# Order of the convolution, the latent heads and the attentions in two hybrid mixers

## The reference

```
z = rmsnorm(x, mix_norm) @ w_in               # 512 tokens x 2680 columns, split into 15 parts
y_a = dsa_mixer(aq, ak, av, iq, ik, iw, ...)  # an index scores keys, the top 128 per query are kept,
                                              # then softmax attention over those (4 heads of 64)
y_b = gla_mixer(bq, bk, bv, bg, br, ...)      # gated linear attention in chunks
y_c = conv_mixer(cu, ...)                     # h = a * sigmoid(gate); 31-tap causal depthwise
                                              # convolution over 256 channels; rmsnorm; silu
y_d = mla_mixer(dcq, dckv, dkpe, ...)         # latent attention: up-projections, head norms, rope
x = x + concat(y_a, y_b, y_c, y_d) @ w_out
```

## Time and profile before

| | us |
|---|---|
| median of 3 runs | 4438.44 (4437.38 to 4439.28) |
| the profiled execution, whole | 4426.43 |
| the profiled execution, span of the core | 4425.2 |
| first mixer, first projection to the end of its attentions | 2452.2 to 2803 |
| second mixer, the same | 3633.2 to 3984 |

### The profile page before, as it was taken

The page is one execution under the profiler, slowest core; times in us unless marked ns, Lnnn a source line. Parts: engine busy times, 40 slices in busy tenths (PEclk is TensorE's granted clock), DMA queues, the critical chain, the costliest instruction groups (busy, mean ns, idle before and its releaser), DMA issues.

```text
span 4425.2 us, 47206 instructions
## 1 busy us (share of the span) xinstructions
PE 4112.5 (93%) x19301; PEld 3236.6 (73%) x19301; DVE 2267.8 (51%) x3544; ACT 1362.8 (31%) x2134; POOL 149.5 (3%) x294
## 2 busy tenths in 40 slices
PE   7659999999999999999999977999999999589999
PEld 6648887666678888887878764788778777467877
DVE  5745898777724444443332488433233325764331
ACT  3243322333333333332221332422232223333221
POOL 8000000000000000000000001000000000100000
PEclk9679999999999999999999986999999999789999
DMA  3002354555566666662333220133323322102332
GB/s 110 1 12 87 110 145 129 164 183 184 183 190 189 190 190 190 190 190 87 95 96 86 62 69 1 53 95 95 100 77 95 96 81 61 46 1 86 95 95 72
DMA packets 253336, 473.56 MB, mean 107 GB/s; under 512 B 15856, under 2 KB 138896, under 8 KB 250944
## 3 DMA queue, kind: packets, MB, share of 16 engines
q1 hardware_dynamic: 253120, 470.53, 35.1%
HBM read 399.96 MB, written 70.52 MB: 106 GB/s over the span
## 4 chain that ended last, share of the span: by engine, by line
PE 79%; DVE 14%; ACT 3%; POOL 2%; issue 1%; DMA 0%; DVEq 0%; ACTq 0%; POOLq 0%; SPq 0%
PE ps L353 23%; PE ps L355 23%; PE ps L354 23%; DVE arena L2656 2%; POOL arena L1139 2%; DVE arena L1825 2%; PE ps L456 1%; PE ps L2223 1%; DVE arena L1139 1%; DVE wlast L344 1%; DVE arena L2751 1%; DVE arena L1821 1%; DVE arena L1822 1%; PE ps L2251 1%; PE ps L2226 1%
## 5 line engine op out<-in xcount | busy, mean ns | idle before, releaser
L344 DVE TENSOR_TENSOR wlast<-wraw,wlast 128x1024 fp32r<-128x1024 f32 x408 | 499.0, 1227 | 799.9 <-ACT wlast L334 799.4
L353 PE MATMUL ps<-XH,wlast 128*128 128x512 f32 (+1 forms) x1904 | 785.4, 412 | 0.7 <-DVE XL L482 0.7
L354 PE MATMUL ps<-XL,wlast 128*128 128x512 f32 (+1 forms) x1904 | 755.4, 397 | 0.0
L355 PE MATMUL ps<-XH,wlast 128*128 128x512 f32 (+1 forms) x1904 | 754.0, 396 | 0.0
L334 ACT ACTIVATE wlast<-wraw 128x1024 fp32r<-128x1024 f32 x408 | 429.4, 1056 | 459.7 <-PE ps L355 444.0
L344 DVE TENSOR_TENSOR wtwo<-wraw,wtwo 128x1024 fp32r<-128x1024 f32 x210 | 258.1, 1230 | 416.9 <-ACT wtwo L334 416.6
L355 PEld LDWEIGHTS ps<-XH,wlast 128*128 128x128 f32 x1904 | 360.3, 189 | 86.5
L353 PEld LDWEIGHTS ps<-XH,wlast 128*128 128x128 f32 x1904 | 360.9, 190 | 74.4 <-issue 3.6
L354 PEld LDWEIGHTS ps<-XL,wlast 128*128 128x128 f32 x1904 | 361.7, 190 | 70.4
L353 PE MATMUL ps<-XH,wtwo 128*128 128x512 f32 (+1 forms) x944 | 383.8, 407 | 0.7 <-DVE XL L482 0.7
L354 PE MATMUL ps<-XL,wtwo 128*128 128x512 f32 (+1 forms) x944 | 368.4, 390 | 0.0
(11 more groups left out here) (460 smaller groups left out, 6542.2 us busy)
## 6 DMA issues: line engine op xcount, KB each, us to landing
wraw<-in_ut SPq DMA_DIRECT2D x128, 512.0 KB, 4.2
wraw<-in_v SPq DMA_DIRECT2D x128, 512.0 KB, 4.0
wraw<-in_ffn_gate SPq DMA_DIRECT2D x88, 512.0 KB, 3.5
wraw<-in_ffn_up SPq DMA_DIRECT2D x88, 512.0 KB, 3.5
wraw<-in_ffn_down SPq DMA_DIRECT2D x88, 512.0 KB, 3.5
acts<-arena SPq DMA_DIRECT2D x128, 256.0 KB, 4.5
gates<-arena SPq DMA_DIRECT2D x16, 2048.0 KB, 9.0
arena<-gates SPq DMA_DIRECT2D x32, 1024.0 KB, 8.3
```

What stands on the lines that cost most here:

```text
L344: ve.e.tensor_tensor(W.items[n][8], W.rawof(n), W.items[n][7], ALU.subtract).then_inc(*ve.up("wlo", n))
L353: mm(out, lh, rh, start=start, stop=False)
L354: mm(out, lh, rl, start=False, stop=False)
L355: return mm(out, ll, rh, start=False, stop=stop)
```

## The change

Four things change, in `plan_mixer`, in the memory of `Mixer.__init__`, in the generators and in the two lists.

1. The projections come in the order cu0, cu2, iq0, iq1, ik, cu1, cu3, aqk and so on: the values and gates of the convolution's first half first.
2. The convolution goes half by half: 31 taps of half 0 (steps c0 to c7), then 31 of half 1 (c8 to c15), each tap waiting for the one before it. c0 may be called from p1 on and takes two steps a round until p4; half 1 starts after p6, with one step a round.
3. The first list runs until p and h are done. The convolution's steps c20 and c21 are called in the first two rounds of the second list; x stands at step 26 by then. In the second list b begins when c is done, and x goes on only when d has passed step 8.
4. QD, KD and the rotary scratch go to the memory lent by the weight ring; the squares QSQ and KSQ to kTd and qTd; UKV and GT to the place of btmp; UQ behind the convolution's scratch. LLa, LLd, PTa, PTd lie over the convolution's memory, so that both attentions' exponentials on ACT wait for the last convolution step (`cn`), and attention a's for the latent queries too (`uqd`).

```
 def plan_mixer(k, l):
+    for m in (0, 2):
+        plan_T(k, ("cu", l, m), w2, 1848 + 128 * m)
     for m in range(2):
         plan_T(k, ("iq", l, m), w2, 768 + 128 * m)
     plan_T(k, ("ik", l), w2, 1024)
-    for m in range(4):
+    for m in (1, 3):
...
+        self.QSQ, self.KSQ = (x.rearrange("p a b -> p (a b)")[:, 0:1536] for x in (self.kTd, self.qTd))
+        L1.at -= 1024
+        self.UKV = L1(512)
+        self.GT = [[L1(4, 16) for _ in range(4)] for _ in range(2)]
...
+        ar.at = at_c
+        LLa, LLd = ([ar(2, 512) for _ in range(2)] for _ in range(2))
+        PTa, PTd = ([ar(512) for _ in range(2)] for _ in range(2))
...
+        e0.at = 4096
+        self.QD, self.KD = e0(4, 4, 96), e0(4, 4, 96)
+        self.RT = [e0(4, 4, 16) for _ in range(4)]
...
-        needs = {"c": 7, "x": 3, "h": 8}
+        needs = {"c": 2, "x": 5, "h": 8}
-        while any(done[b] < steps[b] for b in "pch"):
-            for b in "pxxh" if done["p"] < 7 else "pcxch":
+        while any(done[b] < steps[b] for b in "ph"):
+            for b in "pcc" if done["p"] < 5 else "pcxxh":
+                if b == "c" and done["c"] >= 8 and done["p"] < 7:
+                    continue
...
     def ve_conv(self):
             ve.after().tensor_tensor(self.H[:, m, 32:544], self.CU[:, m, :], self.CU[:, 2 + m, :],
-                                     ALU.mult).then_inc(*ve.up("ch", l, m))
-        for j in range(31):
-            for m in range(2):
+                                     ALU.mult).then_inc(*ve.up())
+            for j in range(31):
...
-                    ve.wait_ge(*at("ct", l, j - 1, m))
-                    v.scalar_tensor_tensor(self.AC[:, m, :], src, wc, self.AC[:, m, :], ALU.mult,
-                                           ALU.add).then_inc(*ve.up("ct", l, j, m))
+                    ve.after().scalar_tensor_tensor(self.AC[:, m, :], src, wc, self.AC[:, m, :], ALU.mult,
+                                                    ALU.add).then_inc(*ve.up())
...
     def order2(self):
-            if done["x"] >= 12 + 9 * min(max((done["a"] - 5) // 4 + 1, 0) // 2, 3):
+            if (done["a"] < 4 or done["c"] == steps["c"]) and done["x"] >= 12 + 9 * min(max((done["a"] - 5) // 4 + 1, 0) // 2, 3):
                 step("a")
-            if done["d"] != self.d_free or done["a"] > 4:
+            if done["d"] != self.d_free or (done["a"] > 4 and done["c"] == steps["c"]):
                 step("d")
-            step("b")
-            if done["b"] * steps["d"] < done["d"] * steps["b"]:
+            step("c")
+            if done["c"] == steps["c"]:
                 step("b")
-            step("x")
+                if done["b"] * steps["d"] < done["d"] * steps["b"]:
+                    step("b")
+            if done["d"] > 8:
+                step("x")
...
     def ac_a(self):
+        ac.wait_ge(*at("cn", l, 1))
+        ac.wait_ge(*at("uqd", l, 3))
         yield from self.att_a.ac()
...
     def ac_d(self):
-        ac.wait_ge(*at("dTd", l, 3, 1))
+        ac.wait_ge(*at("cn", l, 1))
         yield from self.att_d.ac()
```

More of the change, by code:

```diff
@@ L2336, in __init__ @@
         self.csq, self.crs = ar(2, 512), ar(512)
+        at_t = ar.at
         self.tmp = ar(4, 4, 64)
@@ L2370, in __init__ @@
                               (self.IDR[:, 0, :], self.MR[:, i, 0:nk], 0)], ("m", l))
[L2372 to L2376, removed]
-        self.TRI, self.ZH = ar(128), ar(128, dt=HF)
[L2378 to L2382, removed]
+        e0.at = 4096
+        self.QD, self.KD = e0(4, 4, 96), e0(4, 4, 96)
+        self.RT = [e0(4, 4, 16) for _ in range(4)]
+        e0.at = 0
+        ar.at = at_t
+        self.UQ = ar(2, 384)
+        self.TRI, self.ZH = ar(128), ar(128, dt=HF)
         self.dsq, self.drs = self.csq, self.crs
@@ L2419, in order1 @@
         assert done["x"] >= 12
-        self.done_x = done["x"]
+        self.done_x, self.done_c = done["x"], done["c"]
         return out
@@ L2425, in merged1 @@
             next(gens[b], None)
-        for b in "pch":
+        for b in "ph":
             assert next(gens[b], "end") == "end", b
@@ L2430, in pe_proj1 @@
         k, l, XH, XL = self.k, self.l, self.XH, self.XL
+        for m in (0, 2):
+            pe_proj(k, ("cu", l, m), XH, XL, 0, 5, parts=("xL", self.norm_n))
+            yield
         for m in range(2):
-            pe_proj(k, ("iq", l, m), XH, XL, 0, 5, parts=("xL", self.norm_n))
+            pe_proj(k, ("iq", l, m), XH, XL, 0, 5)
             yield
@@ L2508, in toks @@
             ac.note("tks", key)
+        for m in (0, 2):
+            even(m // 2, ("cu", l, m), self.CU[:, m])
+            yield
         for m in range(2):
@@ L2521, in ac_proj1 @@
         yield
-        for m in range(4):
-            even(m, ("cu", l, m), self.CU[:, m])
+        for m in (1, 3):
+            even(m // 2, ("cu", l, m), self.CU[:, m])
             yield
@@ L2564, in odd @@
                 ve.note("pj", key)
+        for m in (0, 2):
+            odd(m // 2, ("cu", l, m), self.CU[:, m])
+            yield
         for m in range(2):
@@ L2570, in ve_proj1 @@
         yield
-        for m in range(4):
-            odd(m, ("cu", l, m), self.CU[:, m])
+        for m in (1, 3):
+            odd(m // 2, ("cu", l, m), self.CU[:, m])
             yield
@@ L2622, in ac_conv @@
             a(self.CU[:, 2 + m, :], self.CU[:, 2 + m, :], ACT.Sigmoid).then_inc(*ac.up("cgate", l, m))
-        for _ in range(16):
-            yield
-        ac.wait_ge(*at("conv", l))
+            for _ in range(8):
+                yield
+        ac.wait_ge(*at("conv", l, 1))
         ac.wait_ge(*at("dss", l))
@@ L2795, in order2 @@
     def order2(self):
-        steps = {"a": self.n_a, "d": self.n_d, "b": self.n_b, "x": 12 + 27}
+        steps = {"a": self.n_a, "d": self.n_d, "b": self.n_b, "x": 12 + 27, "c": 22}
         done = dict.fromkeys(steps, 0)
-        done["x"] = self.done_x
+        done["x"], done["c"] = self.done_x, self.done_c
         out = []
@@ L2824, with merged2 @@
     n_b = 5 + 4 * 11 + 4 + 1
-    def merged2(self, gens, index):
-        gens["x"] = index
+    def merged2(self, gens):
         for b in self.order2():
@@ L2934, in ac_d @@
             a(self.QD[:, i].rearrange("p h e -> p (h e)"), o, ACT.Copy, scale=r).then_inc(*ac.up("qd", l, i))
-            a(self.dtmp[:, i].rearrange("p h e -> p (h e)"), o, ACT.Square, scale=r).then_inc(*ac.free(("uq", l, i)))
+            a(self.QSQ[:, 384 * i:384 * i + 384], o, ACT.Square, scale=r).then_inc(*ac.free(("uq", l, i)))
             ac.note("dhsq", l, i)
@@ L3324, in sp @@
         k, l = self.k, self.l
+        for m in (0, 2):
+            load(k, ("cu", l, m))
         for m in range(2):
```

42 lines of the change are left out of this document (19 added, 23 removed).

## The result

| | before | after |
|---|---|---|
| median of the runs beside each other | 4437.91 us (4433.86 to 4439.28, 6 runs) | 4420.95 us (4418.07 to 4425.13, 6 runs) |
| profiled execution | 4426.43, span 4425.2 | 4420.54, span 4419.3 |
| ratio after to before | | 0.9963, 95% interval 0.995 to 0.9976 |

The change makes the kernel faster by 0.37%, 17 us where 30 were forecast: inside the range, at 57% of the gain. A later comparison gave the same ratio (0.9963, 0.995 to 0.9977).

What follows compares the result with a forecast made beforehand. In each mixer DVE is idle early and owes work late, which holds PE up twice. A net gain of 15 us a mixer, 30 in all, takes the median from 4438.4 to 4408 us; range 4388 to 4428.

Steps and rivals of the forecast that it cites:

- Part 1: Last projection: the 10.84 us PE idle and low-clock matmuls behind it go, 14.2 us less 2.5, so it comes 11.7 earlier.
- term of 2.5 us: Last projection: loss set against the 14.2 us, as x2 to x5 stand behind ACT's sigmoid or aqk evacuations.
- Rival B: Index scores stuck behind DVE's chained taps in p6 to p10: 15.5 us lost, gain about 0, 4438 us; chance 0.08.
- The price of the chained taps: Convolution on DVE: 60 taps cost 0.12 us more each, 7.1 us, covered by DVE's idle time before 2600.
- Part 2: After the last projection: DVE comes free for the next stage at 2622.9 instead of 2635.36, gain 12.4 us.
- Part 3: Stretch to first latent scores: 62.8 us instead of 74.3, including 7 for bare waits; scores come 24 us earlier.
- Rivals A and D: A: front's waits all bare, 5 us a mixer, 4428, chance 0.12. D: full clock or covered waits, 25, 4388, chance 0.12.
- Part 4: First latent scores to last mask: 42.6 us instead of 33.6, mask 15 us earlier; net gain 15 us a mixer.
- PE's lead (+3): At the last mask: PE stands up to three rounds further on in the list, worth 0 to 6 us, taken as 3.
- the clock (-3): Behind the last mask: some 6 us of full-speed work at half clock, costing 3 us net, between 0 and 9.
- wrong in part 4 if PEclk is under 0.9 for more than 10 us: Sign of failure behind the last L2767, one of three; the forecast fails as a whole if two hold.

Runs made afterwards that it cites:

- the kernel with the filler behind the mask: Kernel after plus twelve 256-column products that compute nothing, ahead of the gated attention's first product behind the last mask: 4427.64 us, 0.9982 of before.
- the kernel without deferral: Kernel after, but the selection (x) goes on from the second list's first round instead of waiting for step 8 of d: 4427.86 us, 0.9989 of before.
- The kernel with the third bank: Kernel after with three PSUM banks for the index's scores and four (instead of five) for the projections: 4408.14 us, 0.9937 of before.
- the fourth with the bank: Kernel after with three index banks, selection not put off, and matmuls that compute nothing in the attentions' front and behind the last mask: 4428.14 us, 0.9987 of before.

## Why the prediction was right in kind and half in size

**Part 1, right in mechanism, its term of 2.5 us mis-sized.** The idle of 10.84 us is gone and L2622 takes half the time, as said; so are the late gates. But the last projection came only 4.1 / 4.7 us earlier instead of 11.7. "Against it I set 2.5 us" for x2 to x5 behind ACT's other work: 14.2 less 4.1 / 4.7 is about 10. I had looked at the waits alone, and they are small (4.1 us, 2.8 before). It is the clock. These are marks 10 to 160 of mixer one, before and after:

```profile
2451.67:2601.67 150.00, 143.06 (x757) 115.11 (x755) 94.66 (x151) 55.92 (x95) 2.28 (x3) 0.98 0.26 74
```

```profile
2455.97:2605.97 150.00, 142.76 (x707) 114.69 (x706) 112.02 (x177) 56.03 (x92) 0.88 (x3) 0.92 0.28 80
```

PE is busy as long in both (143.1 and 142.8 us) and issues 50 matmuls fewer. A mean clock of 0.92 for 0.98 over 150 us is about 9 us of full-speed work less, of the 10 that are missing; 28.7 of these microseconds, from 2555.0, ran at 0.82. The low stretches lie among the index's matmuls and their 0.69 us waits; that the waits bring the clock down fits the rows but isn't shown. Rival B's waits behind the taps did not occur. And 4.5 of the 10 us are not fixed by the code ahead: the kernel with the filler behind the mask has the same code up to there and a last projection at 177.2.

**The price of the chained taps, right.** 0.78 us a tap as read from one pair of rows, and about 6 us of the 7.1 where the cover is missing. The Trainium skill (VectorE: DVE Perf Modes, The DRAIN you can't avoid) says of eight copies that a semaphore after each costs nothing extra. Here every tap signals in both orders, so this isn't the same comparison: what costs 0.12 us a tap is waiting for the operation just before it instead of the one before that.

**Part 2, wrong by what part 1 lost.** (A double round by its own terms is 2.51 us and not 2.45, which is 0.3 us over five of them.) DVE's split at 2635.36 came 4.9 us earlier by the marks instead of 12.4. The late projection left DVE idle for 10.69 us before bq's copy, ahead of work that was ready, and that idle is where its 7.5 us are.

**Part 3, right and a little better.** From there to the latent scores 60.6 us for the 62.8 forecast: so the bare waits cost about 5 of the 7 I took. The gates alone are a poorer mark: 1.2 us earlier in mixer one, since the convolution's last step (1.4 us) and a wait of 1.68 us for the gates' product now stand between the split and them. With part 2's loss the scores came 18.7 / 22.6 us earlier instead of 24. Rivals A and D are out.

**Part 4, the mask right within the loss, the clock's price mis-sized.** The last mask came 8.5 / 12.8 us earlier for 15. Behind it the prediction had PE's lead (+3) and the clock (-3) cancel. From last mask to last product the kernel before takes 61.0 us, the one after 64.0 / 69.2: 3 and 8 us lost. The gated attention's first product parts the two terms. It comes 2.3 us behind the mask, for 4.5 before: PE's lead is worth 2.2 us. From there the same 315 matmuls take 61.7 / 67.0 us for 56.5: the clock costs 5.2 / 10.5 us, where I took 3 and at most 9. The clock is 0.50 for 13.7 us behind the last mask in mixer one and for 25.5 us in mixer two, so the line "wrong in part 4 if PEclk is under 0.9 for more than 10 us" came true in both; it is the only sign of being wrong that did. A hole of 6.6 / 7.6 us stands there because L3235 is queued on DVE behind the last mask. That the loss is the clock's doing, and not DVE's, two things show: DVE is busy 19.9 us in that stretch in every kernel, and with the filler it takes 56.4 us again in both mixers. That the hole is what brings the clock down isn't shown, for the kernel without deferral has no such hole in mixer one and 0.67 there. The Trainium skill (TensorE: Matmul & The Clock Gate, Part 1) says that the throttled state is the default and that activity releases it; the trace agrees as far as that, with 0.50 where PE had just stood idle and 1.00 after it had worked on.

**The sum.** Mixer one: 8.5 - 3.0 = 5.5 us; mixer two: 12.8 - 8.2 = 4.6; forecast 15 each. Nearly all of the shortfall is the granted clock in two places and what follows from the first: the 2.5 us of part 1 were about 10, and the 3 us of part 4 were 5.2 and 10.5. The profiles' mixers give 10 us and the medians 17 in both comparisons; the 7 us between I can't place. The stretches outside the mixers vary by 9 us from one execution of a program to the next, so two single profiles can't place them. By the mixers alone the change gave a third of the forecast; that the program's time lies inside the range owes 7 us to something that I did not predict.

**The best version.** The kernel with the third bank has the lowest median, 4408.1 (0.9937), then 4410.1 and 4411.1, both with the bank too. Its interval just overlaps that of the kernel after (0.9954 against 0.995), and the fourth with the bank, with all fillers and no deferral, had 4428. I would take it, for its time and not for a mechanism I can show.

## What to carry to other kernels

When a reorder trades one long idle of TensorE for several short waits, price the matmuls behind each short wait at the low clock too: here stretches with 4 us of such waits lost about 10. To see what the clock costs, find a stretch with the same number of matmuls in every kernel and compare its length: here 315 of them took 56.5, 61.7 and 67.0 us. Price a chain on VectorE by the distance of its starts, not by mean durations, and check that other work covers it. And before reading a shift of a few us out of two profiles, profile one kernel twice: see which stretches repeat to a few tenths and which wander.

## What the runs showed of the hardware that I had not expected

- The granted clock's course is a property of the program more than of the execution: the two profiles of the kernel after have the same marks within 0.7 us in 358, while a kernel whose edit comes at mark 290 differs by 4.5 us at mark 180. Where DVE paces, the clock's course may differ without a trace in the marks: from mark 279.6 to 293.2 of mixer one the mean is 0.75 in one profile and 0.62 in the other.
- The same 315 matmuls at a mixer's end took 56.4 to 56.5 us at a clock of 0.98 to 1.00, 61.7 at 0.91 and 67.0 at 0.83. One program can have both: without the deferral mixer one took 62.4 us (0.86) and mixer two 56.5 (1.00).
- Matmuls that compute nothing can pay, and need not: 7 to 8 us of them ahead of the critical product gave back 5.2 us in one mixer and 10.5 in the other. Where the clock was at 1.00 already, they cost about 5 us a mixer.
